# FFN input projections of a float32 encoder block: two of eight k-pairs by seven products of block sums

## The reference, cut to what matters

```
h = x + 1/2 * SwiGLU_1(RMSNorm(x));  mixing;  cross attention;  h = h + 1/2 * SwiGLU_2(RMSNorm(h));  out = RMSNorm(h)
def swiglu(x, w_in, w_out):
    gate, up = jnp.split(x @ w_in, 2, axis=-1)
    return (jax.nn.silu(gate) * up) @ w_out
```

## Time and profile before

| | |
|---|---|
| median of 3 runs | 2148.61 us (2148.19 to 2149.09) |
| span of the profiled execution, first to last instruction | 2145.7 us |
| PE busy | 2137.6 us (100%), 9585 matmuls |
| weight loads into PE | 1774.9 us (83%) |
| DVE busy | 1192.2 us (56%) |
| ACT busy | 1010.0 us (47%) |
| POOL busy | 39.0 us (2%) |
| DMA | 468.15 MB, mean 218 GB/s |

### The profile page before, as it was taken

How to read it: one execution, slowest core, us unless ns; L and a number is a source line. 1 busy time by engine, 2 the same in 40 slices (tenths; PEclk the granted TensorE clock), 3 DMA queues, 4 the chain that set the end, 5 groups by cost and what they waited for, 6 DMA issues and landing times.

```text
span 2145.7 us, 26770 instructions
## 1 busy us (share of the span) xinstructions
PE 2137.6 (100%) x9585; PEld 1774.9 (83%) x9585; DVE 1192.2 (56%) x1187; ACT 1010.0 (47%) x1157; POOL 39.0 (2%) x50
## 2 busy tenths in 40 slices
PE   9999999999999999999999999999999999999998
PEld 8888888888888888888888888888888888888887
DVE  6555555555555576566555656665555555554444
ACT  6444444443444465456544555554444444444343
POOL 0000000000000031000000000000000000000000
PEclk9999999999999999999999999999999999999999
DMA  8766677666666677765587766676676666765554
GB/s 317 240 217 213 212 226 220 213 210 194 226 218 212 217 266 240 237 213 185 177 285 239 234 207 186 201 241 216 211 230 214 212 211 225 223 212 191 194 187 157
DMA packets 183139, 468.15 MB, mean 218 GB/s; under 512 B 16928, under 2 KB 67488, under 8 KB 182944
## 3 DMA queue, kind: packets, MB, share of 16 engines
q1 hardware_dynamic: 180912, 459.91, 67.2%
q0 software_dynamic: 1728, 6.82, 0.9%
q10 hardware_dynamic: 432, 0.53, 0.1%
HBM read 439.41 MB, written 27.79 MB: 218 GB/s over the span
## 4 chain that ended last, share of the span: by engine, by line
PE 99%; issue 0%; DMA 0%; DVE 0%; ACT 0%; POOLq 0%; DVEq 0%; POOL 0%
PE acc L1640 32%; PE acc L1642 32%; PE acc L1643 32%; PE acc L1754 1%; PE aux L1937 0%; PE aux L1910 0%; PE aux L1906 0%; PE aux L1933 0%; PE aux L1932 0%; PE aux L1905 0%; PE aux L1847 0%; DMA arrived<-in_first_cols 0%; PE acc L1719 0%; PE acc L1717 0%; PE acc L1715 0%
## 5 line engine op out<-in xcount | busy, mean ns | idle before, releaser
L1052 DVE TENSOR_TENSOR w_lo<-raw,w_hi 128x1024 fp32r<-128x1024 f32 x765 | 935.9, 1227 | 884.1 <-ACT w_hi L629 882.8
L629 ACT ACTIVATE w_hi<-raw 128x1024 fp32r<-128x1024 f32 x765 | 808.1, 1060 | 1043.1 <-PE acc L1643 1014.4
L1640 PE MATMUL acc<-w_hi,a_hi 128*128 128x512 f32 x1384 | 539.0, 389 | 0.0
L1642 PE MATMUL acc<-w_lo,a_hi 128*128 128x512 f32 x1384 | 538.5, 389 | 0.0
L1643 PE MATMUL acc<-w_hi,a_lo 128*128 128x512 f32 x1384 | 538.5, 389 | 0.0
L1640 PE MATMUL acc<-w_hi,b_hi 128*128 128x512 f32 x1216 | 474.5, 390 | 0.0
L1642 PE MATMUL acc<-w_lo,b_hi 128*128 128x512 f32 x1216 | 473.2, 389 | 0.0
L1643 PE MATMUL acc<-w_hi,b_lo 128*128 128x512 f32 x1216 | 473.2, 389 | 0.0
L1640 PEld LDWEIGHTS acc<-w_hi,a_hi 128*128 128x128 f32 x1384 | 259.8, 188 | 54.7 <-issue 0.9
L1643 PEld LDWEIGHTS acc<-w_hi,a_lo 128*128 128x128 f32 x1384 | 259.8, 188 | 54.1
L1642 PEld LDWEIGHTS acc<-w_lo,a_hi 128*128 128x128 f32 x1384 | 259.8, 188 | 53.5
(11 more groups left out here) (195 smaller groups left out, 687.6 us busy)
## 6 DMA issues: line engine op xcount, KB each, us to landing
raw<-in_ffn_w_in SPq DMA_DIRECT2D x349, 512.0 KB, 4.2
raw<-in_ffn_w_out SPq DMA_DIRECT2D x176, 512.0 KB, 4.2
raw<-in_w_mix_in SPq DMA_DIRECT2D x80, 512.0 KB, 4.6
raw<-in_w_ckv SPq DMA_DIRECT2D x64, 512.0 KB, 4.4
memq<-bounce SPq DMA_DIRECT2D x196, 128.0 KB, 3.8
bounce<-stage SPq DMA_DIRECT2D x37, 512.0 KB, 5.0
raw<-in_w_mix_out SPq DMA_DIRECT2D x32, 512.0 KB, 4.7
raw<-in_w_cq SPq DMA_DIRECT2D x32, 512.0 KB, 4.3
```

The lines of the kernel that those rows point to most:

```text
L629: eng.activation(w_hi[:, u % RING], raw[:, u % RING], ACT.Copy).then_inc(w_hi_done, 1)
L1052: eng.tensor_tensor(w_lo[:, u % RING], raw[:, u % RING], w_hi[:, u % RING].bitcast(f32), ALU.subtract).then_inc(w_lo_done, 1)
L1640: eng.matmul(dst, x_hi[:, rows], w_hi[:, slot, i], start=start and i == 0, stop=False)
L1642: eng.matmul(dst, x_hi[:, rows], w_lo[:, slot, i], start=False, stop=False)
```

## The change

A chunk pair is now walked by k-pairs: k-pair kp is 256 rows of weights x (512 gate + 512 up columns). The weight array is laid out anew on the host, so that a unit is 128 rows x (gate | up), 512 KB as before, and k-pair kp is units 2kp and 2kp + 1. Token tiles x k blocks make a 2 x 2 matrix of blocks X, and k blocks x (gate, up) a 2 x 2 matrix W. Six k-pairs are multiplied as before, by 8 block products (two **steps** of 12 matmuls). K-pairs 1 and 4 (`SEVEN_AT`) are multiplied by 7 products of sums of blocks (Winograd's form of Strassen's algorithm), 21 matmuls in four steps of 6, 3, 6 and 6. So a chunk pair has 16 + 4 = 20 steps, and each step takes one of the four slots of `w_hi` and `w_lo`; the `raw` ring still counts 16 units.

What this needs: sums of x blocks once for each FFN (`x_sums`, five DVE operations, and a high and a low half, in chunk pair 0); for each of the two k-pairs three DVE operations for sums of weight blocks (`sum_first` 1024 wide, `sum_third` and `sum_fourth` 512 wide, into `sigma`); products that belong to several results go to `aux` and `tp`, and `mix` (one ACT copy, four DVE operations of 512) combines them into `comb_g` and `comb_u`; at the end of the chunk pair `final` (four DVE operations of 512) adds them to the four banks of `acc`. Silu and hidden then read from SBUF. PE takes the banks in the order 1, 0, 2, 3, the last k-pair bank by bank (`plain_last`), and at the start of the next chunk pair waits for each bank's `final` (for hidden, after chunk pair 0).

`turn` now goes to SBUF (`turned_hid`), since `tp` is in use. New tensors lie over `h`, over the last part of `hid_hi`/`hid_lo` and over `row_gain`; so `h` is loaded again in four transfers of 512 KB in each FFN's output part, and the loads of `row_gain` wait until the input part is done. Chunk pair 0 keeps its products.

```diff
+SEVEN_AT = (1, 4)
+NS = len(SEVEN_AT)
+STEP_AT = [2 * kp + 2 * sum(s < kp for s in SEVEN_AT) for kp in range(U8)]
+PAIR_STEPS = 2 * U8 + 2 * NS
...
@@ SyncE
                 with eng.Fori(1, FJ) as j:
-                    chunk(w, 2 * U8 * j, base + 2 * U8 * j)
-                    chunk(w, 2 * U8 * j + U8, base + 2 * U8 * j + U8, first=base == FFN1_IN,
-                          late=(number(TURNS, hid) - 1 + j, stage[:], hid_done, silus[base] + j))
+                    for n in range(2 * U8):
+                        if n == U8:
+                            send(number(TURNS, hid) - 1 + j, stage[:], hid_done, silus[base] + j)
+                        if n == U8 + 2:
+                            fetch(number(TURNS, hid) - 1 + j, base == FFN1_IN)
+                        before = unit_step(n - RING) if n >= RING else n - RING
+                        eng.wait_ge(w_lo_done, pair_base(base, j) + before + 1)
+                        eng.dma_start(raw[:, n % RING].rearrange("p k n -> p (k n)"),
...
@@ ScalarE
+                def seven(j, kp):
...
+                    eng.activation(w_hi[:, step % RING], diagonal(kp), ACT.Copy).then_inc(w_hi_done, 1)
+                    slot_free(j, step + 1)
+                    eng.activation(w_hi[:, (step + 1) % RING, 0], raw[:, (n + 1) % RING, 1], ACT.Copy
+                                   ).then_inc(w_hi_done, 1)
+                    eng.wait_ge(combined, sums + 1)
+                    slot_free(j, step + 2)
+                    eng.activation(w_hi[:, (step + 2) % RING], sigma[:, 0:2], ACT.Copy).then_inc(w_hi_done, 1)
+                    eng.wait_ge(combined, sums + 3)
+                    slot_free(j, step + 3)
+                    eng.activation(w_hi[:, (step + 3) % RING], sigma[:, 2:4], ACT.Copy).then_inc(w_hi_done, 1)
...
@@ VectorE
+                def pair(j, hi, lo):
+                    plain(j, 0)
...
+                        final(base, j - 1, 1)
+                        sum_first(j, 1)
+                        final(base, j - 1, 0)
+                        sum_third(j, 1)
+                        final(base, j - 1, 2)
+                        sum_fourth(j, 1)
+                        final(base, j - 1, 3)
+                        seven_raw(j, 1)
+                        hidden_final(base, rs, hid, j - 1)
+                    seven_sums(j, 1)
+                    plain(j, 2)
+                    plain(j, 3)
+                    sum_first(j, 4)
+                    eng.wait_ge(t_read, split_number(hid) - 1 + j)
+                    turn(number(TURNS, hid) - 1 + j, turned_hid[:])
+                    sum_third(j, 4)
+                    eng.wait_ge(t_hi, split_number(hid) + j)
+                    eng.tensor_tensor(lo, turned_hid[:], hi.bitcast(f32), ALU.subtract).then_inc(t_read, 1)
+                    sum_fourth(j, 4)
+                    seven_raw(j, 4)
+                    seven_sums(j, 4)
+                    plain(j, 5)
+                    plain(j, 6)
+                    mix(j)
+                    plain(j, 7)
...
@@ TensorE
+                def seven(j, kp):
...
+                    ready(j, step)
+                    product(aux[:, 0], x11, (slot[0], 0), start, stop)
+                    product(acc[:, 0], n4, (slot[0], 1)).then_inc(w_used, 1)
+                    ready(j, step + 1)
+                    product(acc[:, 2], x12, (slot[1], 0)).then_inc(w_used, 1)
+                    ready(j, step + 2)
+                    product(aux[:, 1], s1, (slot[2], 0), start, stop)
+                    product(tp_banks[:, 1], s3, (slot[2], 1), start, stop).then_inc(w_used, 1)
+                    ready(j, step + 3)
+                    product(tp_banks[:, 0], s2, (slot[3], 0), start, stop)
+                    product(acc[:, 3], x22, (slot[3], 1)).then_inc(w_used, 1)
```

More of the change, by code:

```diff
@@ L152, in slot_loads @@
     while at < base:
+        if any(first + 2 * U8 <= at < last for first, last in ((FFN1_IN, FFN1_OUT), (FFN2_IN, FFN2_OUT))):
+            n += 2 * U8 // RING
+            at += PAIR_STEPS
+            continue
         length = U22 if FFN1_OUT <= at < MIX_IN or at >= FFN2_OUT else U8
@@ L584, in _ @@
             load_mem(3)
[L586 to L589, removed]
             rstd_of("mem", NT)
@@ L706, in silu, with loaded @@
                     last.then_inc(silu_done, 1)
[L708 to L717, removed]
+                def loaded(j, n):
+                    count = slot_loads(base + 2 * U8, n % RING) + n // RING - 2 * U8 // RING
+                    eng.wait_ge(w_loaded[n % RING], 16 * count + 16 + 16 * (2 * U8 // RING) * j)
@@ L1137, in hidden, with low @@
                     last.then_inc(hid_done, 1)
[L1139 to L1151, removed]
+                def low(j, step, src, blocks=UK):
+                    eng.wait_ge(w_hi_done, pair_base(base, j) + step + 1)
+                    eng.tensor_tensor(w_lo[:, step % RING, 0:blocks], src,
+                                      w_hi[:, step % RING, 0:blocks].bitcast(f32), ALU.subtract
+                                      ).then_inc(w_lo_done, 1)
@@ new lines, in plain, with loaded, sums_made @@
+                def plain(j, kp):
+                    for half in range(2):
+                        low(j, STEP_AT[kp] + half, raw[:, (2 * kp + half) % RING])
+                def loaded(j, n):
+                    count = slot_loads(base + 2 * U8, n % RING) + n // RING - 2 * U8 // RING
+                    eng.wait_ge(w_loaded[n % RING], 16 * count + 16 + 16 * (2 * U8 // RING) * j)
+                def sums_made(j, kp):
+                    return combineds[base] + 3 * NS * (j - 1) + 3 * SEVEN_AT.index(kp)
@@ new lines, in bank_free, with ready, plain @@
+                def bank_free(j, bank):
+                    if isinstance(j, int):
+                        eng.wait_ge(*((silu_done, hid_done)[bank // 2], silus[base] + 1))
+                    else:
+                        eng.wait_ge((gate_final, up_final)[bank // 2],
+                                    gate_finals[base] + 2 * (j - 2) + (2, 1, 1, 2)[bank])
+                def ready(j, step):
+                    eng.wait_ge(w_lo_done, pair_base(base, j) + step + 1)
+                def plain(j, kp):
+                    for half in range(2):
+                        step = STEP_AT[kp] + half
+                        ready(j, step)
+                        for bank in (1, 0, 2, 3):
+                            if kp == 0 and half == 0:
+                                bank_free(j, bank)
+                            last = product(acc[:, bank], tile(2 * kp + half, bank % 2),
+                                           (step % RING, bank // 2), start=kp == 0 and half == 0)
+                        last.then_inc(w_used, 1)
@@ new lines, in plain_last @@
+                def plain_last(j):
+                    step = STEP_AT[U8 - 1]
+                    ready(j, step + 1)
+                    for bank in (1, 0, 2, 3):
+                        for half in range(2):
+                            last = product(acc[:, bank], tile(2 * U8 - 2 + half, bank % 2),
+                                           ((step + half) % RING, bank // 2), stop=half == 1)
+                            if bank == 3:
+                                last.then_inc(w_used, 1)
+                        if bank != 3:
+                            last.then_inc(bank_full, 1)
@@ L2019, in units, with pairs @@
                          for col, u in places])
+    def pairs(name, cols):
+        w = turned_rows(name, inputs[name][0]).reshape(-1, P, 2 * FF)
+        return np.stack([np.concatenate([w[k, :, col:col + CH] for col in cols[2 * j:2 * j + 2]], axis=1)
+                         for j in range(1, FJ) for k in range(KT)])
     def chunks(cols, length=U8):
```

289 lines of the change are left out of this document (245 added, 44 removed).

## The result

| | before | after |
|---|---|---|
| median | 2148.85 us (2148.19 to 2149.87, 4 runs) | 2233.91 us (2228.16 to 2238.23, 4 runs) |
| span of the profiled execution | 2145.7 us | 2226.1 us |
| matmuls | 9585 | 9465 |

The change makes the kernel slower by 85 us: ratio 1.0394, 95% interval 1.0374 to 1.0414. The forecast was 2164 us in 2130 to 2194. The sign was right, and the place; the size was over five times too small (+15 forecast, +85 measured).

A forecast was written before the change was run, and what follows sets the result against it. PE, busy for the whole span at the full clock, was taken to bound the kernel. -27.2 + 42 + 0.8 = +15.6 us on a span of 2145.7 gave 2161.3, against the median of the runs 2164 us, range 2130 to 2194.

The forecast's parts named there:

- Removed: PE in the looped chunk pairs of both FFNs: 120 matmuls fewer, all on the path, 27.2 us saved.
- The 0.8 us for chunk pair 0's hidden: After chunk pair 0, PE waits at bank 2 for hidden: 0.4 us once per FFN, 0.8 us.
- DVE's load: DVE's work in a looped chunk pair: 34.7 us of 42.2, over 80%, which fits as a sum.
- The seam: Start of the next chunk pair: final(3) ends just before PE needs bank 3, 0.1 us to spare; costed at 0.
- Step 10: K-pair 4: PE waits for the chain behind unit 9 and the fetch, 2.1 us, 20 times, 42 us.
- the 5.7 us: K-pair 4: serial chain on DVE and ACT from the turn's start until PE can start step 10, 5.7 us.
- The clock: PE after a pause: each microsecond of work at 1.2 GHz would cost 0.5 us; not in the sum.
- (b): Late landings, 4.1 us stall at step 10, seam slips too, clock may fall: 2214 us, half-way 2190; chance 0.14.
- (a): Transfers land sooner, so step 10's stall is 1.4 us (2150 us) or 0.5 us (2132 us); chance 0.30.
- (c): No stall at all, DVE and DMA both on time: 2122 us; chance 0.08.

The follow-up runs named there:

- e6: e5 with the fetch ahead of load 12 instead of load 10; 2123.54 us, 0.9884.
- e1: The changed kernel with the turn, its high half and its low half moved from between k-pair 4's sums to behind its split steps; 2144.02 us, 0.9981.
- e2: e1 with step 10's low half ahead of k-pair 4's two short sums and step 11's behind them; 2143.39 us, 0.9976.
- e3: e1 with the fetch ahead of load 12 instead of load 10; 2142.00 us, 0.9967.
- e5: e2 with mix behind the two low halves of k-pair 7 instead of ahead of them; 2124.98 us, 0.9891.
- e9: e1 with mix behind the low halves of k-pair 7, without e2's edit; 2127.60 us, 0.9901.
- e8: The changed kernel with only the fetch moved, ahead of load 12 instead of load 10; 2284.78 us, 1.0632.
- e7: The changed kernel with only mix moved, behind the low halves of k-pair 7; 2226.58 us, 1.0365.
- e4: The changed kernel with 14 matmuls of a zero tile ahead of step 10 in each of the 20 looped pairs; 2199.35 us, 1.0246.

## Why the prediction was right or wrong

**Removed, 27.2 us: right.** e6 shows 24.9 us of it. The 0.8 us for chunk pair 0's hidden are right too: PE's first matmul on bank 2 comes 0.4 us late once in each FFN. So is DVE's load: 35.8 us of the pair shown against 34.7 laid out. ACT got 71 us in all, 3.6 a pair and not 7, and it was rightly priced at nothing.

**The seam: right.** final(3) was laid out 0.1 us ahead of its need and no PE wait on it shows in the changed kernel. It was right for a reason I had not written down: the stall holds PE back by 2.4 to 6.0 us, and in that time DVE and the loads catch up. In e1 and e2, with the stall gone, PE waited for final(2) or final(3) 31 and 28 times. That part was luck. My sentence that mix "is needed only at the next k-pair 1" looked at who waits for mix, not at what stands behind it on DVE: two low halves, and behind them two loads.

**Step 10, the step that failed: the landing times.** "its last transfer issued at 12.7 ... took 4.0 to 6.7 us ... median 4.7 ... So it lands at T + 17.4, turn starts 17.45." Measured: the issue times held (load 9 at T + 10.7, the last fetch transfer at T + 12.8), the last transfer took 6.5 us in the pair shown, where the turn starts at T + 19.35, and 6.2 in the mean. Unit 9, at "4.2 (median) to 5.3 us", took 6.0 in the median. From the turn onward the 5.7 us held to 0.1. With 6.2 in place of 4.7 the sum gives a stall of 3.6 us, 72 us in all, where the prediction had 42; 74.5 were measured. So the term "PE stands for 2.1 us" was mis-sized, by the landing times in it. In the changed kernel the two landings come close together: unit 9's sum would have held the turn to T + 18.8 with any fetch, and the turn waited only another 0.55 us in this pair and 1.0 on the mean (19.7 us in 20) for the fetch. I took landings from a kernel in which one load stood within 3 us of the fetch, and used them where two loads stand within 1.7 us ahead and two right behind. For the fetch the numbers of the rows were not wrong, they belonged to another traffic. For unit 9 they were also poorly read: 5.3 us is one load ahead of one fetch, and the 20 of them in that trace took up to 6.5. What makes transfers land later in the denser traffic stays open but for the 1.2 us that e3 shows, and no run moved the fetch ahead of loads 8 and 9, so what an earlier fetch alone gives back was not measured.

**The clock, left out of the forecast: 30 us.** The prediction named it inside rival (b) at 0.5 us per microsecond and put nothing of it into the sum, because no pause in the rows could show it. It is the second part of the miss: 74.5 - 42 = 32.5 us came from the stall and 30.5 from this. Here the four shortest stalls (2.4 to 2.9 us beyond the pitch) left the granted clock at 1.00 and cost 0.1 us more each, the next matmul at 0.34 us. The stall shown (3.9 us beyond the pitch) was followed by eight matmuls at 0.40 to 0.56 us: 1.7 us on top. The sentence cited from the Trainium skill, "TensorE: Matmul & The Clock Gate" (Part 1), that idleness lets the clock fall to half, agrees with these rows.

**The rivals.** (a) fell: no last transfer of a looped fetch was quicker than 4.7 us. The estimate from the fit of the Trainium skill's page "DMA: Bandwidth & Descriptors" (Anatomy of one DMA), 3.2 us for 512 KB, comes near load 8 (3.5 us) and misses load 9 (6.7). The page gives its fit per transfer, for those that GpSimd issues; these are SP's, with others in flight. (b) had the long landing and the falling clock right and its mechanism, the seam, wrong. (c) fell for this order, and is what e5 and e6 measure once turn and mix stand elsewhere: 2122 was its time, 2123.5 came out in e6. The upper end of my range, 2194, was taken half-way into (b), though the bounds of the landing time gave a stall of 4.1 us, 82 us in 20 pairs, or 2204 us, by my own sum: the range did not contain its own bounds.

## What to carry to other kernels

Take out work from the engine that bounds the run only after asking, for each operation that is put in a row on another engine, what stands behind it in that row, not only who waits for it: here a transposition that nothing waited for in its chunk pair, placed between two sums, cost 90 us (e1), and a combination that nobody needed for another 5 us or more cost 16 to 18 (e1 to e9, e2 to e5). A transfer's landing time belongs to the traffic around it; where the change bunches transfers, take the longest landing of the rows, not the median (here 6.7 us, which prices the stalls at 82 us; the median gave 42, and 74.5 were measured). And a stall of TensorE can cost more than its length: here some 30 us of slower matmuls came on top of 74.5 us of stalls.

## What the runs showed of the hardware that was not expected

A transfer is held up by transfers issued behind it. With the fetch's four transfers moved from behind load 9 to behind load 11, load 9 landed in 4.9 us in the median instead of 6.1 (e1 and e3) and in 4.7 instead of 6.0 (the changed kernel and e8), while load 8 stayed at 3.4 to 3.5 in all four. Load 10 then stands 1.1 us behind load 9, where the fetch stood 0.5 us behind it. How the queue brings this about, and whether the fetch's distance or its kind matters, these runs do not show.

The clock's fall is not gradual in these rows: matmuls are 0.23 or 0.43 us apart with one or two in between, and the pace changed back within a seven of k-pair 4 (by 264.2 us). Nor does it fall only while PE stands: behind the stall that ended at 1767.93 us the low level begins 1.5 us after PE is back at work. The length of a stall does not decide it by itself either. In the changed kernel the four stalls of 2.4 to 2.9 us beyond the pitch left the clock at 1.00 and the 16 of 3.0 to 6.0 us did not. But in e7 one of 2.95 us was followed by a fall and one of 3.08 us was not, and in e4 one of 2.3 us was. Matmuls with a zero tile kept the clock up as well as useful ones (e4, mean 0.998).

PE's start behind even a short wait costs a little beyond the wait: the second matmul comes 0.34 us behind the first and not 0.23, at the full clock too (e2, and the four short stalls of the changed kernel).
